# Filter transforms of a two-block kernel in plain fp32, with a reordered opening

## The reference

```python
mod_x = silu(c) @ mod_w + mod_b                     # 6 x 1024: shifts, scales, gates
hx = x * (1 + sc1) + sh1
ox = multiscale_pool(hx, pool_w, pool_scale)        # window means minus hx, then 4 group products
x = layer_norm(ALPHA * x + g1 * ox)
x = layer_norm(ALPHA * x + g2 * swiglu(x * (1 + sc2) + sh2))
# block two: MLA attention + conv FFN, then Hyena + conv FFN
h = sin(freq * (... sin(freq * (z @ fw1 + fb1)) ...))   # three sine layers, width 64
filt = (h @ fw_out) * decay                              # 512 x 2 orders x 2 directions x 1024
k_f = rfft(two_sided_kernel(filt_fwd, filt_bwd), n=1024)
y = irfft(rfft(z) * k_f)                                  # later, in the Hyena mixer
```

## Time and profile before

| | |
|---|---|
| median of 3 runs | 1887.74 us (1886.28 to 1888.52) |
| profiled execution | 1892.42 us |
| its span, first to last instruction | 1891.1 us |
| mean granted TensorE clock | 0.974 |
| busy: TensorE, VectorE, GpSimd, ScalarE | 94%, 53%, 41%, 33% |
| chain that ended last | TensorE 78%, VectorE 13% |
| from HBM and to it | 183.58 MB, 12.58 MB |

### The profile page before, as it was taken

How to read it: one execution, slowest core, us unless ns; L and a number is a source line. 1 busy time by engine, 2 the same in 40 slices (tenths; PEclk the granted TensorE clock), 3 DMA queues, 4 the chain that set the end, 5 groups by cost and what they waited for, 6 DMA issues and landing times.

```text
span 1891.1 us, 19650 instructions
## 1 busy us (share of the span) xinstructions
PE 1775.0 (94%) x7796; PEld 1420.2 (75%) x7796; DVE 1001.1 (53%) x1378; ACT 630.5 (33%) x889; POOL 784.6 (41%) x364
## 2 busy tenths in 40 slices
PE   3588999999999899999999999999998999999997
PEld 1455888888877666778888888778887788888785
DVE  7787643331244757374444413588997554444124
ACT  1333322222134545253333322442333343333222
POOL 3554344444443311243444444356563434444442
PEclk9798999999998999999999999999999999999998
DMA  8672533233231201122223232522222322332322
GB/s 307 231 256 89 179 100 98 92 100 99 91 99 59 73 31 37 45 69 99 94 96 101 90 100 91 188 89 101 79 84 84 101 78 90 100 101 90 99 90 78
DMA packets 54342, 197.45 MB, mean 104 GB/s; under 512 B 6216, under 2 KB 6664, under 8 KB 52393
## 3 DMA queue, kind: packets, MB, share of 16 engines
q1 hardware_dynamic: 52584, 190.05, 30.3%
q10 hardware_dynamic: 1666, 6.14, 1.0%
HBM read 183.58 MB, written 12.58 MB: 104 GB/s over the span
## 4 chain that ended last, share of the span: by engine, by line
PE 78%; DVE 13%; issue 2%; POOL 2%; ACT 2%; DMA 2%; SPq 0%; DVEq 0%; ACTq 0%
PE ps L491 25%; PE ps L493 25%; PE ps L492 24%; DVE mod_ring L1686 1%; POOL filter_taps_lo L1528 1%; PE ps L864 1%; DVE x_residual L2138 1%; POOL w_lo L1501 1%; DVE x_residual L2129 1%; DMA n_values<-in_hy_fw_out 1%; DVE n_values L1844 1%; PE ps L638 1%; DMA mod_ring<-in_mod_t 1%; DVE x_tokens L1686 1%; DVE x_residual L2125 1%
## 5 line engine op out<-in xcount | busy, mean ns | idle before, releaser
L1501 POOL TENSOR_TENSOR w_lo<-w_raw,w_hi 128x1024 fp32r<-128x1024 f32 x244 | 597.4, 2449 | 850.9 <-ACT w_hi L1056 850.9
L491 PE MATMUL ps<-act_hi,w_hi 128*128 128x512 f32 x1348 | 532.4, 395 | 18.7 <-POOL w_lo L1501 8.0
L492 PE MATMUL ps<-act_lo,w_hi 128*128 128x512 f32 x1348 | 528.6, 392 | 0.0
L493 PE MATMUL ps<-act_hi,w_lo 128*128 128x512 f32 x1348 | 528.4, 392 | 0.0
L1056 ACT ACTIVATE w_hi<-w_raw 128x1024 fp32r<-128x1024 f32 x248 | 262.8, 1060 | 787.4 <-PE ps L493 775.1
L491 PEld LDWEIGHTS ps<-act_hi,w_hi 128*128 128x128 f32 x1348 | 255.4, 189 | 77.3 <-POOL w_lo L1501 7.8
L492 PEld LDWEIGHTS ps<-act_lo,w_hi 128*128 128x128 f32 x1348 | 255.5, 190 | 53.8 <-issue 0.7
L493 PEld LDWEIGHTS ps<-act_hi,w_lo 128*128 128x128 f32 x1348 | 255.3, 189 | 53.9
L491 PE MATMUL ps<-f_hidden_hi,w_hi 128*128 128x512 f32 x528 | 207.9, 394 | 1.9 <-POOL w_lo L1501 1.9
L493 PE MATMUL ps<-f_hidden_hi,w_lo 128*128 128x512 f32 x528 | 207.6, 393 | 0.0
L492 PE MATMUL ps<-f_hidden_lo,w_hi 128*128 128x512 f32 x528 | 206.0, 390 | 0.0
(11 more groups left out here) (269 smaller groups left out, 2481.3 us busy)
## 6 DMA issues: line engine op xcount, KB each, us to landing
w_raw<-in_w_stream SPq DMA_DIRECT2D x258, 512.0 KB, 3.7
mod_ring<-in_mod_t SPq DMA_DIRECT2D x23, 512.0 KB, 6.4
x_tokens<-in_mod_t SPq DMA_DIRECT2D x17, 512.0 KB, 6.7
spectra<-filter_spectra SPq DMA_DIRECT2D x16, 512.0 KB, 3.8
hy_filter<-spectra SPq DMA_DIRECT2D x8, 1024.0 KB, 4.8
mod_ring_late<-in_mod_t SPq DMA_DIRECT2D x8, 512.0 KB, 4.8
x_residual<-in_xT ACTq DMA_DIRECT2D x8, 256.0 KB, 7.3
x_tokens<-in_x_tokens SPq DMA_DIRECT2D x1, 2048.0 KB, 7.9
```

The lines of the kernel that those rows point to most:

```text
L491: PE.matmul(o, lh, rh, start=start, stop=False, **kw)
L492: PE.matmul(o, lh, rl, start=False, stop=False, **kw)
L493: return PE.matmul(o, ll, rh, start=False, stop=stop, **kw)
L1501: GP.tensor_tensor(low, B.WR[:, c % 2, :], f32(high), ALU.subtract).then_inc(S.w_lo, 1)
```

## The change

It does these things, all before the first FFN.

- The filter transforms take the taps and the table as they are, in plain fp32: one matmul in place of three. The split of taps and table on ScalarE and GpSimd is gone. The raw table has a place of its own and is loaded behind the decay.
- The taps have two places, by the unit's parity; `decays(v)` waits for the transforms of unit v - 2.
- Modulation has nine slots, five own (`mod_ring`, `mod_ring_more`) and four shared; the eight late tiles use three of the shared ones.
- The order on all five queues is written anew: the first sum of output weights comes after sine layer two and the second after layer three; tiles stand between decays; taps 7 stand before the columns of the norm.

```diff
-        self.flt = sb("filter_taps", [P, 4, T])
+        self.flt = sb("filter_taps", [P, 2, 4, T])
         odd_at = sb.at
         self.odd = sb("odd_spectrum", [P, 2, T])
         self.kspec = sb("filter_spectra", [P, 2, 4, T])
-        filter_at = sb.at
-        self.flh = sb("filter_taps_hi", [P, 4, T], F32R)
-        self.fll = sb("filter_taps_lo", [P, 4, T], F32R)
-        self.x_tok = sb("x_tokens", [P, 4, D])
+        self.x_tok = sb("x_tokens", [P, MOD_SHARED, D])
+        self.MW2 = sb("mod_ring_more", [P, MOD_OWN - 3, D])
         assert sb.at <= nc.sbuf_usable_end
-        own, shared = [self.MW[:, i, :] for i in range(3)], [self.x_tok[:, i, :] for i in range(4)]
-        turned = own[2:] + own[:2]
-        sb = Place(nc, filter_at)
-        self.mod_late = sb("mod_ring_late", [P, 4, D])
-        late = [self.mod_late[:, i, :] for i in range(4)]
-        self.mod_slots = (own + shared, turned, turned + shared, late)
+        self.mod_slots = ([self.MW[:, i, :] for i in range(3)] + [self.MW2[:, i, :] for i in range(MOD_OWN - 3)] +
+                          [self.x_tok[:, i, :] for i in range(MOD_SHARED)])
...
-        self.tabr = self.WR[:, :, :].rearrange("p s (b m) -> p (s b) m", m=P)
-        self.tabh, self.tabl = (t[:, 4:8, :].rearrange("p k (b m) -> p (k b) m", m=P) for t in (self.AH, self.AL))
+        self.tab = Place(nc, table_at)("dft_table", [P, 16, P])
...
-MOD_SLOTS = (7, 3, 7, 4)
-MOD_RINGS = (0, 16, 22, MOD_LATE, 48)
+MOD_OWN, MOD_SHARED = 5, 4
...
+    own, every = MOD_OWN, MOD_OWN + MOD_SHARED
+    slots = [t % every for t in range(own + every)] + [t % own for t in range(10)]
+    slots += [(own + t) % every for t in range(MOD_LATE - len(slots))] + [own + t % 3 for t in range(48 - MOD_LATE)]
...
-            PE.wait_ge(S.flt_lo, 4 * v + TAP_ORDER.index(q) + 1)
-            ins = mm3(ps[:, bank, :], B.tabh[:, b, :], B.tabl[:, b, :], B.flh[:, q, :], B.fll[:, q, :],
-                      k == 0, k == 1)
+            PE.wait_ge(S.decayed, 4 * v + TAP_ORDER.index(q) + 1)
+            ins = PE.matmul(ps[:, bank, :], B.tab[:, b, :], B.flt[:, v % 2, q, :], start=(k == 0), stop=(k == 1))
...
-        PE.wait_ge(S.fw_sums, 2)
+        PE.wait_ge(S.fw_sums, 1)
         PE.wait_ge(S.skip_in, 16)
         taps(0)
-        for v in range(4):
-            taps(v + 1)
-            if v == 2:
-                PE.wait_ge(S.diff, 8)
-            elif v == 3:
-                PE.wait_ge(S.x_ready, 4)
-            unit(v)
-            if v == 1:
-                pool_windows()
-            elif v in (2, 3):
-                pool_linear(v - 2, v)
+        PE.wait_ge(S.fw_sums, 2)
+        taps(1)
+        PE.wait_ge(S.dft_in, 16)
+        unit(0)
+        taps(2)
+        unit(1)
+        taps(3)
+        unit(2)
+        pool_windows()
+        taps(4)
+        PE.wait_ge(S.diff, 8)
+        unit(3)
+        pool_linear(0, 3)
         taps(5)
+        PE.wait_ge(S.x_ready, 4)
+        unit(4)
+        pool_linear(1, 4)
+        taps(6)
         first_norm_mean()
         PE.wait_ge(S.x_ready, 8)
-        unit(4)
-        taps(6)
         unit(5)
+        taps(7)
         PE.wait_ge(S.ln_centred, 8)
         PE.wait_ge(S.sq_added, 7)
         columns(0, B.sq_sum, True).then_inc(S.ln_turned, 1)
-        taps(7)
         unit(6)
...
-        SC.dma_start(B.tabr, B.a["dft_fwd"]).then_inc(S.dft_in, 16)
         SC.dma_start(B.decay[:, :, :], B.a["decay"][0]).then_inc(S.decay_in[0], 16)
+        SC.dma_start(B.tab[:, :, :], B.a["dft_fwd"]).then_inc(S.dft_in, 16)
...
-        for v in range(4):
-            filter_hi(v)
-            if v == 1:
-                SC.wait_ge(S.x_in, 16 * KD)
-                SC.wait_ge(S.affine, 1)
-                SC.wait_ge(S.fw_sums, 2)
-                for k in range(KD):
-                    SC.activation(B.hx[:, k, :], X[:, k, :], ACT.Identity, bias=B.MOD[:, k:k + 1],
-                                  scale=B.AFF[:, 0, 0, k:k + 1]).then_inc(S.pool_in, 1)
-            elif v == 2:
-                w_hi(0)
-                for k in range(4):
-                    diff_whole(k)
-                    diff_hi(k)
-                w_hi(1)
-            odd_part(v, 0)
-            odd_part(v, 1)
-            if v == 2:
-                for k in range(4, KD):
-                    diff_whole(k)
-                for k in range(KD):
-                    SC.activation(X[:, k, :], X[:, k, :], ACT.Copy, scale=ALPHA_1).then_inc(S.x_scaled, 1)
-                for k in range(4, KD):
-                    diff_hi(k)
+        odd_part(0, 0)
+        odd_part(0, 1)
+        odd_part(1, 0)
+        odd_part(1, 1)
+        w_hi(0)
+        w_hi(1)
+        odd_part(2, 0)
+        SC.wait_ge(S.x_in, 16 * KD)
+        SC.wait_ge(S.affine, 1)
+        SC.wait_ge(S.fw_sums, 2)
+        for k in range(KD):
+            SC.activation(B.hx[:, k, :], X[:, k, :], ACT.Identity, bias=B.MOD[:, k:k + 1],
+                          scale=B.AFF[:, 0, 0, k:k + 1]).then_inc(S.pool_in, 1)
+        odd_part(2, 1)
+        for k in range(4):
+            diff_whole(k)
+            diff_hi(k)
+        for k in range(4, KD):
+            diff_whole(k)
+        odd_part(3, 0)
+        for k in range(KD):
+            SC.activation(X[:, k, :], X[:, k, :], ACT.Copy, scale=ALPHA_1).then_inc(S.x_scaled, 1)
+        odd_part(3, 1)
+        for k in range(4, KD):
+            diff_hi(k)
+        odd_part(4, 0)
+        odd_part(4, 1)
...
-        GP.wait_ge(S.dft_hi, 1)
-        GP.tensor_tensor(B.tabl[:, :, :], B.tabr, f32(B.tabh[:, :, :]), ALU.subtract).then_inc(S.dft_lo, 1)
-        def filter_lo(v):
-            for at, q in enumerate(TAP_ORDER):
-                GP.wait_ge(S.flt_hi, 4 * v + at + 1)
-                GP.tensor_tensor(B.fll[:, q, :], B.flt[:, q, :], f32(B.flh[:, q, :]),
-                                 ALU.subtract).then_inc(S.flt_lo, 1)
...
+        w_lo(0)
+        w_lo(1)
+        pool_lo(0)
+        pool_lo(1)
...
             if layer == 0:
                 kept_rows()
-            if layer < 2:
+                VE.wait_ge(S.silu_c, 1)
+                mod_tiles(0, 1)
+            else:
                 VE.wait_ge(S.fw_out_in, 16)
                 VE.wait_ge(S.fsd_cleared, 1)
-                VE.tensor_tensor(B.fsd[0:HY_W, layer, :, :], B.fwo[:, :, 0], B.fwo[:, :, 1],
-                                 (ALU.add, ALU.subtract)[layer]).then_inc(S.fw_sums, 1)
-            VE.wait_ge(S.silu_c, 1)
-            mod_tiles(*((0, 1), (1, 3), (3, 6))[layer])
+                VE.tensor_tensor(B.fsd[0:HY_W, layer - 1, :, :], B.fwo[:, :, 0], B.fwo[:, :, 1],
+                                 (ALU.add, ALU.subtract)[layer - 1]).then_inc(S.fw_sums, 1)
...
         def decays(v):
             VE.wait_ge(S.decay_in[v // 4], 16)
-            for at, q in enumerate(TAP_ORDER):
-                VE.wait_ge(S.taps, 4 * v + at + 1)
-                if v:
-                    VE.wait_ge(S.flt_lo, 4 * v - 3 + at)
+            if v >= 2:
+                VE.wait_ge(S.spectrum, 4 * v - 4)
+            for at in range(4):
+                decay_tile(v, at)
...
+        VE.wait_ge(S.hid, 3)
+        VE.wait_ge(S.decay_in[0], 16)
+        for at in range(4):
+            decay_tile(0, at)
+            mod_tiles(at + 1, at + 2)
+        decays(1)
+        mod_tiles(5, 8)
+        butterfly(0)
+        decays(2)
+        mod_tiles(8, 13)
+        butterfly(1)
+        mod_tiles(13, 16)
+        decays(3)
+        butterfly(2)
+        for k in range(KD):
+            difference(k)
+        mod_tiles(16, 20)
+        decays(4)
+        mod_tiles(20, 24)
+        butterfly(3)
+        pooled_tiles(0)
         decays(5)
-        mod_tiles(low + 3, high)
+        mod_tiles(24, 28)
+        butterfly(4)
+        pooled_tiles(1)
+        mod_tiles(28, 32)
+        decays(6)
+        mod_tiles(32, 34)
...
-        decays(7)
+        mod_tiles(34, MOD_LATE)
         butterfly(6)
...
+    every = MOD_OWN + MOD_SHARED
+    modulation(0, every)
     SP.dma_start(B.ident[:, :], a["identity"]).then_inc(S.ident_in, 16)
-    modulation(7, 17)
-    SP.wait_ge(S.mod_used, 14)
+    modulation(every, every + MOD_OWN)
+    spectrum_out(0)
+    SP.wait_ge(S.mod_used, every)
     SP.dma_start(B.x_tok[:, :, :], a["x_tokens"]).then_inc(S.x_tok_in, 16)
-    modulation(17, 19)
-    SP.wait_ge(S.dft_lo, 1)
-    fetch(0)
-    fetch(1)
-    for v in range(8):
-        if 1 <= v < 4:
-            modulation(*((19, 25), (25, 34), (34, 40))[v - 1])
-        spectrum_out(v)
-        if v == 2:
-            SP.wait_ge(S.decayed, 16)
-            SP.dma_start(B.decay[:, :, :], a["decay"][1]).then_inc(S.decay_in[1], 16)
-        elif v == 3:
-            fetches(2, 4)
-        elif v == 5:
-            fetches(4, 6)
-        elif v == 6:
-            modulation(MOD_LATE, MOD_LATE + 4)
-            fetches(6, 8)
+    fetches(0, 2)
+    modulation(14, 18)
+    spectrum_out(1)
+    modulation(18, 21)
+    SP.wait_ge(S.decayed, 16)
```

(16 more changed lines are left out.)

147 lines of the change are left out of this document (51 added, 96 removed).

## The result

| | before | after |
|---|---|---|
| median | 1887.01 us of 4 runs (1884.87 to 1888.52) | 1866.28 us of 4 runs (1858.76 to 1868.01) |
| profiled execution, its span | 1892.42, 1891.1 | 1864.57, 1863.3 |
| FFN's first matmul | 193.67 | 164.76 |
| from there to the end of the span | 1697.4 | 1698.5 |
| mean granted clock | 0.974 | 0.983 |

The ratio is 0.987, 95% interval 0.9846 to 0.9894: faster, by 20.7 us in the medians (which alone would give 0.989). The kernel once more, in five runs beside others, gave 0.9878. The opening, up to the FFN's first matmul, is 28.9 us shorter in the traces; the medians show 8.2 us less than that, and the part on the stretch behind the opening says what is known of the difference.

The account below looks back on a forecast made before the run. An opening chain of waits before a saturated TensorE was taken as the bound; gains walked up to 32.7 us at the FFN, and 1892.4 less 32 gave 1860, 1856 on the median's scale; range 1846 to 1871.

Parts of the forecast that it names:

- the supply rival: Modulation's loads in the opening stay at 187 GB/s, 4.2 MB take 12 us more: gain 20, 1868 us; chance 0.18.
- What bounds: Whole kernel: the opening is a chain of waits before a saturated TensorE, so its loss counts one for one.
- Unit prices: Filter transforms: eight fp32 products at 0.88 us, 7.0 a unit instead of 5.6; TensorE gains 11 us over eight units.
- The 5 us charged back: VectorE's modulation tiles: four or five stretched by 1.05 us beside GpSimd's remaining splits, taken off a 17 us saving.
- To unit 0: Opening up to the end of the first transform unit: 34.0 to 41.0 us, before 54.8; gain 13.8 us.
- To the differences: Opening up to the end of the eight differences: 79.1 us, before 95.5; affine ready at 61.3; gain 16.3 us.
- The new wait: ScalarE: eight affine copies precede unit 2's second odd copy, delaying it to 67.7 us; eats some 4 us of TensorE.
- To the centring and the scaling: Centring ends at 129.8 us, before 155.4, gain 25.6; norm's scaling at 152.9, before 184.77, gain 31.9.
- To the FFN: Unit 7 after butterfly 6, 7.0 us plus about 1 of half clock: FFN at 161, before 193.67; gain 32.7.
- The sum: Whole kernel: profiled 1892.4 us less 32 is 1860; with that execution 4.7 over the median, 1856 on the median's scale.
- Clock: TensorE's 116 us of opening work stays at clock 0.86, 19 us more: gain 17, 1871 us; chance 0.14.
- Slower by half clock throughout: Opening: fp32 transforms at half clock, 116 us become 232, FFN starts at 274, whole kernel 1969 us; chance 0.03.

Follow-up runs that it names:

- half transforms: The changed kernel with only the second of each two products of every filter transform: median 1865.00 us, 0.9871 of the time before the change, FFN's first matmul at 168.06.

## Why the prediction was right, and where it was off

The sign, the range (1846 to 1871) and the mechanism of the opening held. The time came 10.3 us over the forecast of 1856: 3.8 in the opening (164.76 for 161) and, by the medians, 6.5 behind it. The time alone is nearer to the supply rival (1868) than to the forecast; it is the walk through the trace, step by step, that speaks for the forecast.

- **What bounds.** Right inside a trace: TensorE is at 300.00 of 300 us between 200 and 500 in both, and of the 28.9 us the two profiled executions show 27.8. "What the opening loses, the kernel loses one for one" doesn't hold for the medians, which show 20.7. The prediction had named "a gain in the opening that is missing from the end" as a sign of being wrong; 8.2 of 28.9 us are missing.
- **Unit prices.** A unit was priced at 7.0 us and took 7.03, a tile alone at 1.21 and took 1.21. The 11 us more for TensorE cost nothing that the half transforms could show. The 5 us charged back for four or five stretched tiles were 8.8 for six (2.00, 3.35, 1.59, 2.30, 3.36, 3.36, less 1.2 each). Beside a whole 128x512 instruction of GpSimd a tile loses 1.1 us, beside a whole chunk 2.15, and I had priced all by the first. The second price stood in the trace of before, where I hadn't read it, on VectorE and GpSimd:

```profile
137.00 3.37 DVE L1686 CUSTOM_DVE_ANT_0 x_tokens<-x_tokens,silu_c_row 128x1024 f32<-128x1024 f32 x1
```
```profile
136.46 6.13 POOL L1501 TENSOR_TENSOR w_lo<-w_raw,w_hi 128x1024 fp32r<-128x1024 f32 x2 [2.76 <-ACT w_hi L1056]
```

Here the page that I weighed (the Trainium skill, SBUF — State Buffer, on two separate sides) was nearer: the loser waits for the whole instruction. It also says that this holds for VectorE instructions with two SBUF inputs; the rows agree, since tiles stretch, and so did the addition of 128x8 (2.37 us for 0.16), while decays and differences, with one operand in PSUM, don't.
- **To unit 0.** It ran from 34.51 to 41.54 for a forecast of 34.0 to 41.0, a gain of 13.3 for 13.8: right.
- **To the differences.** They ended at 81.05 for 79.1. The affine came at 64.9 for 61.3: tile 14 was read at 59.10, and both tiles were stretched by the two chunks, 2.9 us, which I had placed elsewhere. The queue moved 350 GB/s between 47 and 59 us, not the 418 of a four-microsecond window. There the figure of the Trainium skill (DMA: Bandwidth & Descriptors, where 436 GB/s comes from), 358 GB/s, is the better one. The new wait at 70.61 was there, 8.12 us on TensorE for my 4; but as a cause it was worth 1 to 2 us, because VectorE's list stood right behind it.
- **To the centring and the scaling.** The centring ended at 133.69 for 129.8: the 2 us carried over, and a tile beside a chunk at 118.56 (3.36 us) that I had not placed. The scaling began at 156.41 for 152.9: carried over; the one tile stretched there was in the sum.
- **To the FFN.** 164.76 for 161: carried over. Of half clock I had allowed 3 us for units 6 and 7; they took 1.5 and 1.7.
- **The sum.** The step that failed most: 1892.4 less 32 (the walk had 32.7), and 4.7 off "on the scale of the median". The profiled execution of before had a long stretch behind it (1697.4). Taking off its distance to the median credited the changed kernel with a stretch of some 1694; its median of 1866.3, less 1.3 around the span and 164.8, has 1700. That is the 6.5.
- **What the change is made of.** The prediction gave the new order, the slots and the fp32 transforms one walk together. The runs split it: fp32 with a second place gives 24.1 of the 28.9 us in the opening; without that place it makes the kernel 20 us slower. New order and nine slots together give the other 4.8; the new order with seven slots is 9.6 us behind the old. The prediction said of the two places that a "wait goes and none takes its place"; it didn't see that the splits had been doing that work before.
- **The rivals.** Supply: VectorE waited 5.1 us for modulation tiles (0.8 of them for tile 0), a hair over the 5 us named as this rival's sign, but 6.0 before; tile 14 was read at 59.1, when tile 15 was expected, and not 12 us later, so as a price it was wrong here. It comes true as soon as two slots go. Clock: 0.93 from 50 us to the FFN, not 0.86. Slower by half clock throughout: no; what did turn slower in the runs was another case, the missing second place, and I had none like it.

## What to carry to other kernels

- When a split or copy is removed, ask what else it did: a copy is also a second buffer. Removing it and adding the second place for its input belong in one edit; here the place was worth more than the work saved.
- Keep VectorE instructions that read two SBUF tensors away from GpSimd's, by placing those with a PSUM operand beside them. The price goes by the length of GpSimd's instruction, even for an addition of 128x8.
- A wait removed in a hand order is worth what the next engine's list, and TensorE's clock behind the next wait, leave of it: here 1 to 2 of 5 us, and 2.1 of 8.9.
- Compare openings in the traces as well as whole times: two traces of one kernel differed by 0.9 us at the end of the opening, its nine executions by 9 us as wholes. But a gain read in the opening alone is not yet one of the kernel; here 20.7 of 28.9 us reached the median.

## What the runs showed of the hardware

- A VectorE instruction with two SBUF inputs that meets one of GpSimd's waits for it: 128x8 took 2.37 us instead of 0.16, a tile 3.36 instead of 1.21, both beside a chunk's split of some 2.4 us. Decays and differences, with one PSUM operand, kept their time.
- Less work on TensorE need not gain time: with 28 us of it gone, the granted clock from 50 us to the FFN was 0.83 instead of 0.93, and the FFN came 3.3 us later.
- The same twelve matmuls took 2.86 us at full clock and up to 5.03 at half, behind waits for VectorE of 2.38 and 6.29 us.
- Loads ran at 418 GB/s over 4 us and at 350 over the 12 us in which they were waited for.
- The stretch behind the opening took one of two sizes in 14 traces, some 7 us apart, with the granted clock lower in more of its windows in the longer.
